# The opening of an encoder layer: first projections in halves of 256 tokens, V's first unit and its fill ahead of the first scores

## The reference, cut to what matters

```python
hn = rmsnorm(x, ln_mix_pre[i])
q, k, v = jnp.split(hn @ w_qkv, 3, axis=-1)          # 16 heads of 64
for blk in range(seq // Q_BLOCK):
    z = jnp.einsum('bhqd,bhkd->bhqk', q[:, :, t0:t1], k[:, :, :t1]) * scale
    log_stay = jnp.where(before, jax.nn.log_sigmoid(-z), 0.0)
    log_pass = lax.cumsum(log_stay, axis=3, reverse=True) - log_stay
    a = jnp.where(before, jnp.exp(jax.nn.log_sigmoid(z) + log_pass), 0.0)
    outs.append(jnp.einsum('bhqk,bhkd->bhqd', a, v[:, :, :t1]))
x = x + rmsnorm(concat(outs) @ w_o, ln_mix_post[i])
x = x + rmsnorm(swiglu_ffn(rmsnorm(x, ln_ffn_pre[i]), w_gu, w_down), ln_ffn_post[i])
```

## Time and profile before

| what | us |
|---|---|
| median of three runs (1438.04 to 1438.3) | 1438.04 |
| the profiled execution's own time | 1431.42 |
| its span | 1429.6 |
| TensorE busy | 1353.5 (95%) |
| VectorE busy | 720.0 (50%) |
| ScalarE busy | 544.1 (38%) |
| GpSimd busy | 377.8 (26%) |

### The profile page before, as it was taken

One profiled execution on the slowest core, in us unless ns is written; L12 is line 12 of the kernel. 1 busy time (PEld: TensorE's weight loads), 2 busy tenths in 40 slices (PEclk: granted clock), 3 DMA queues, 4 the chain that ended last, 5 costly groups with the idle time before them and its releaser, 6 DMA issues.

```text
span 1429.6 us, 17837 instructions
## 1 busy us (share of the span) xinstructions
PE 1353.5 (95%) x6528; PEld 1121.9 (78%) x6528; DVE 720.0 (50%) x881; ACT 544.1 (38%) x964; POOL 377.8 (26%) x244
## 2 busy tenths in 40 slices
PE   5999999999999967996999999999999999999995
PEld 4788888888888856785788888888888888888884
DVE  6489989899898994323212130313132222313148
ACT  5577767677776762332221112021212111111213
POOL 5111011101111051551252323142323232232326
PEclk9999999999999978997999999999999999999998
DMA  5000000000000032120011101020211111110102
GB/s 191 31 30 16 31 30 30 29 15 30 30 30 15 16 103 74 63 70 0 30 59 44 60 30 59 29 73 15 73 44 53 50 44 44 44 59 29 59 15 118
DMA packets 18335, 66.64 MB, mean 47 GB/s; under 512 B 2032, under 2 KB 2032, under 8 KB 18288
## 3 DMA queue, kind: packets, MB, share of 16 engines
q1 hardware_dynamic: 16560, 59.78, 12.1%
q10 hardware_dynamic: 1728, 6.29, 1.3%
HBM read 61.87 MB, written 4.19 MB: 46 GB/s over the span
## 4 chain that ended last, share of the span: by engine, by line
PE 91%; DVE 6%; ACT 1%; DMA 1%; POOL 0%; issue 0%; POOLq 0%; ACTq 0%; DVEq 0%
PE bank L1152 11%; PE bank L1151 11%; PE bank L1153 11%; PE bank L1001 6%; PE bank L1003 6%; PE bank L1002 6%; PE bank L1199 5%; PE bank L1198 5%; PE bank L1200 5%; PE bank L1102 4%; PE bank L1076 2%; PE bank L1078 2%; PE bank L1122 2%; PE bank L1121 2%; PE bank L1050 2%; PE bank L1052 2%
## 5 line engine op out<-in xcount | busy, mean ns | idle before, releaser
L693 POOL TENSOR_TENSOR w_lo<-raw,w_hi 128x1024 fp32r<-128x1024 f32 x89 | 216.1, 2432 | 746.1 <-ACT w_hi L438 745.9
L1151 PE MATMUL bank<-hnT_hi,w_hi 128*128 128x512 f32 x704 | 277.4, 394 | 2.9 <-DVE hnT_lo L794 2.9
L1152 PE MATMUL bank<-hnT_lo,w_hi 128*128 128x512 f32 x704 | 278.8, 396 | 0.0
L1153 PE MATMUL bank<-hnT_hi,w_lo 128*128 128x512 f32 x704 | 276.4, 393 | 0.0
L934 DVE TENSOR_TENSOR sg<-bank,sg 128x512 f32<-128x512 f32 x44 | 30.4, 692 | 439.3 <-ACT sg L626 439.3
L438 ACT ACTIVATE w_hi<-raw 128x1024 fp32r<-128x1024 f32 x89 | 93.3, 1059 | 404.2 <-PE bank L1153 353.5
L874 DVE TENSOR_TENSOR_SCAN stay<-stay,diag_one 128x256 f32<-128x256 f32 (+7 forms) x128 | 189.8, 1483 | 5.8 <-ACT stay L554 5.8
L948 DVE TENSOR_TENSOR y<-bank,y 128x512 f32<-128x512 f32 x176 | 119.3, 690 | 94.4 <-PE bank L1200 93.1
L1151 PEld LDWEIGHTS bank<-hnT_hi,w_hi 128*128 128x128 f32 x704 | 133.1, 189 | 34.7 <-DVE hnT_lo L794 3.5
L1153 PEld LDWEIGHTS bank<-hnT_hi,w_lo 128*128 128x128 f32 x704 | 133.0, 189 | 29.9
L1152 PEld LDWEIGHTS bank<-hnT_lo,w_hi 128*128 128x128 f32 x704 | 132.9, 189 | 29.2
(11 more groups left out here) (97 smaller groups left out, 2018.5 us busy)
## 6 DMA issues: line engine op xcount, KB each, us to landing
raw<-in_units SPq DMA_DIRECT2D x98, 512.0 KB, 3.2
acc<-in_x SPq DMA_DIRECT2D x8, 512.0 KB, 8.6
x_in<-in_x ACTq DMA_DIRECT2D x8, 512.0 KB, 3.4
out<-y SPq DMA_DIRECT2D x7, 512.0 KB, 2.6
g_pre_s<-in_mix_pre ACTq DMA_DIRECT2D x1, 512.0 KB, 5.5
g_post_t<-in_mix_post ACTq DMA_DIRECT2D x1, 512.0 KB, 4.2
g_ffn_t<-in_ffn_pre ACTq DMA_DIRECT2D x1, 512.0 KB, 3.7
g_out<-in_ffn_post ACTq DMA_DIRECT2D x1, 512.0 KB, 3.8
```

Source lines behind the costliest of these rows:

```text
L693: nc.gpsimd.tensor_tensor(w_lo[slot], raw[:, raw_slot, :], w_hi[slot].bitcast(F32), ALU.subtract).then_inc(w_ready, 1)
L1151: nc.tensor.matmul(bank_ap, wh, hnT_hi[:, kt, cols], start=(kt == 0), stop=False)
L1152: nc.tensor.matmul(bank_ap, wh, hnT_lo[:, kt, cols], start=False, stop=False)
L1153: mm = nc.tensor.matmul(bank_ap, wl, hnT_hi[:, kt, cols], start=False, stop=(kt == KT - 1))
```

## The change

1. SyncE issues `g_pre_s` behind the first tile (it was ScalarE's first instruction), k's unit behind it and q's behind the second tile; the other six tiles follow.
2. ScalarE splits k's unit after the first tile's squares (was the fourth's), q's after the third's (was the seventh's) and V's after the sixth's (was after the third projection).
3. The low parts of these three units are made by VectorE, after it has scaled tiles 0, 2 and 6, and no longer by GpSimd.
4. Each of the four first projections is done in two halves of 256 tokens (`project_first`), 24 matmuls of 256 columns each; `FIRST_PARTS` and `FIRST_TILES` are rewritten for pairs (projection, half), so that a half follows the transposes of tiles 2 to 7 and two follow the last.
5. V's first unit lies in a slot of its own, the chunk buffers `AT_hi` and `AT_lo`, unused until slot 7.
6. In the first step the seven parts of slots 0 to 2 all stand ahead of slot 0's scores.

```diff
--- before.py
+++ after.py
@@ -182,10 +182,16 @@
     return UNIT_OFF[kind] % 2 if first else (UNIT_OFF[kind] + par) % 2
 
 
-def fill_parts(s):
-
-    parts = [("vkq"[n // 16], n % 16 // 8, n % 8) for n in range(PARTS_UPTO[s], PARTS_UPTO[s + 1])]
-    return parts[:1], parts[1:]
+def fill_parts(s, first):
+
+
+
+    upto = PARTS_UPTO[s + 1]
+    if first and s < 3:
+        upto = PARTS_UPTO[3]
+    parts = [("vkq"[n // 16], n % 16 // 8, n % 8)
+             for n in range(PARTS_UPTO[3] if first and s in (1, 2) else PARTS_UPTO[s], upto)]
+    return (parts, []) if first and s == 0 else (parts[:1], parts[1:])
 
 
 ACC_END = acc_base(PAIRS - 1) + 2
@@ -207,11 +213,9 @@
 
 FIRST_ACC = [("k", 0), ("q", 1), ("k", 1), ("q", 0)]
 
-FIRST_PARTS = {3: [(0, range(0, 2))], 4: [(0, range(2, KT))], 6: [(1, range(0, 5))],
-               7: [(1, range(5, KT))],
-               NT: [(2, range(KT)), (3, range(KT))]}
-
-FIRST_TILES = [4, 6, 8, 8]
+
+FIRST_PARTS = {2: [(0, 0)], 3: [(3, 0)], 4: [(0, 1)], 5: [(1, 0)], 6: [(2, 0)], 7: [(1, 1)], NT: [(2, 1), (3, 1)]}
+FIRST_TILES = [(2, 4), (4, 6), (6, 8), (2, 8)]
 
 
 
@@ -345,9 +349,11 @@
 
             return k_b[:, par, :] if h else k_a[:, par, :]
 
-        w_hi = [w_hi01[:, 0, :], w_hi01[:, 1, :], w_hi2[:, :], hnT_hi[:, 0, :]]
-        w_lo = [w_lo01[:, 0, :], w_lo01[:, 1, :], w_lo2[:, :], hnT_lo[:, 0, :]]
-        LAST_SLOT = 3
+
+
+        w_hi = [w_hi01[:, 0, :], w_hi01[:, 1, :], w_hi2[:, :], hnT_hi[:, 0, :], AT_hi.rearrange("p a n -> p (a n)")]
+        w_lo = [w_lo01[:, 0, :], w_lo01[:, 1, :], w_lo2[:, :], hnT_lo[:, 0, :], AT_lo.rearrange("p a n -> p (a n)")]
+        LAST_SLOT, FIRST_V_SLOT = 3, 4
 
         x_tile = [sem(f"x_tile{t}") for t in range(NT)]
         raw_in = [sem("raw_in0"), sem("raw_in1")]
@@ -406,12 +412,12 @@
 
         @block.sync
         def _(sp):
-            for t in range(4):
+            for t in range(NT):
                 sp.dma_start(acc[:, t, :], x_tiles[:, t, :]).then_inc(x_tile[t], 16)
-            sp.dma_start(raw[:, 0, :], units[0]).then_inc(raw_in[0], 16)
-            for t in range(4, NT):
-                sp.dma_start(acc[:, t, :], x_tiles[:, t, :]).then_inc(x_tile[t], 16)
-            sp.dma_start(raw[:, 1, :], units[1]).then_inc(raw_in[1], 16)
+                if t == 0:
+                    sp.dma_start(g_pre_s[:, :], g_mix_pre.partition_broadcast(P)).then_inc(gain_in, 16)
+                if t < 2:
+                    sp.dma_start(raw[:, t, :], units[t]).then_inc(raw_in[t], 16)
             for n in range(2, UNITS1):
                 sp.wait_ge(w_ready, n - 1)
                 sp.dma_start(raw[:, n % 2, :], units[unit_row(n)]).then_inc(raw_in[n % 2], 16)
@@ -445,7 +451,6 @@
                 act.wait_ge(t_full, index + 1)
                 nc.scalar.activation(out_ap, in_ap, ACT.Copy).then_inc(t_hi, 1)
 
-            act.dma_start(g_pre_s[:, :], g_mix_pre.partition_broadcast(P)).then_inc(gain_in, 16)
 
 
             def start_hi(t):
@@ -460,10 +465,12 @@
                     act.wait_ge(sq_done, t)
                 nc.scalar.activation(junk_s[:, :], acc[:, t, :], ACT.Square,
                                      accum_out=ss[:, t:t + 1]).then_inc(sq_done, 1)
-                if t == 3:
+                if t == 0:
                     split_hi(0, 0, 0, 16)
-                if t == 6:
+                if t == 2:
                     split_hi(1, 1, 1, 16)
+                if t == 5:
+                    split_hi(2, FIRST_V_SLOT, 0, 32)
                 if t >= 2:
                     start_hi(t - 2)
             start_hi(NT - 2)
...
@@ -704,10 +709,6 @@
             for t in range(NT):
                 pool.wait_ge(sq_done, t + 1)
                 inverse_rms(t, t)
-                if t == 3:
-                    split_lo(0, 0, 0)
-            split_lo(1, 1, 1)
-            split_lo(2, 0, 0)
 
             def step(p, par, first=False, proj=True):
                 for s in range(SLOTS):
@@ -804,6 +805,8 @@
                 nc.vector.memset(q_lo2[OTHER[h], h, :].bitcast(F32), 0.0).then_inc(zeros, 1)
             dve.wait_ge(consts, 5)
             dve.wait_ge(gain_in, 16)
+
+            FIRST_SPLIT = {0: (0, 0), 2: (1, 1), 6: (2, FIRST_V_SLOT)}
             for t in range(NT + 1):
                 if t < NT:
                     dve.wait_ge(rstd_done, t + 1)
@@ -812,6 +815,11 @@
                     nc.vector.scalar_tensor_tensor(out=hn_s[:, t % 2, :], in0=acc[:, t, :],
                                                    scalar=rstd[:, t:t + 1], in1=g_pre_s[:, :],
                                                    op0=ALU.mult, op1=ALU.mult).then_inc(hn_ready, 1)
+                if t in FIRST_SPLIT:
+                    n, slot = FIRST_SPLIT[t]
+                    dve.wait_ge(w_hi_ready, n + 1)
+                    nc.vector.tensor_tensor(w_lo[slot], raw[:, n % 2, :], w_hi[slot].bitcast(F32),
+                                            ALU.subtract).then_inc(w_ready, 1)
                 if t:
                     norm_lo(2 * t - 2, t - 1, 0)
                     norm_lo(2 * t - 1, t - 1, 1)
@@ -991,6 +999,26 @@
 
         @block.tensor
         def _(pe):
+            def project_first(n, b):
+
+                kind, c = FIRST_ACC[n]
+                slot = "kq".index(kind)
+                first_col = (0, 6 * P)[b] if (kind, c) == ("q", 0) else 2 * P * ((1 if kind == "q" else 2 * c) + b)
+                cols = slice(first_col, first_col + 2 * P)
+                dst = FIRST_ACC_B[n][:, 2 * P * b:2 * P * (b + 1)]
+                pe.wait_ge(w_ready, slot + 1)
+                pe.wait_ge(t_lo, 2 * FIRST_TILES[n][b])
+                for kt in range(KT):
+                    wh = w_hi[slot][:, kt * P:(kt + 1) * P]
+                    wl = w_lo[slot][:, kt * P:(kt + 1) * P]
+                    nc.tensor.matmul(dst, wh, hnT_hi[:, kt, cols], start=(kt == 0 and b == 0), stop=False,
+                                     skip_group_check=True)
+                    nc.tensor.matmul(dst, wh, hnT_lo[:, kt, cols], start=False, stop=False, skip_group_check=True)
+                    mm = nc.tensor.matmul(dst, wl, hnT_hi[:, kt, cols], start=False,
+                                          stop=(kt == KT - 1 and b == 1), skip_group_check=True)
+                if b:
+                    mm.then_inc(acc_full, 1)
+
             def project_tiles(kind, c, slot, kts, dst):
 
                 out_ap = dst[:, :].rearrange("p (g n) -> p g n", n=2 * P) if kind == "q" and c == 0 else dst[:, :]
@@ -1020,12 +1048,8 @@
                     pe.wait_ge(hn_ready, t + 1)
                     for half in range(2):
                         transpose_norm(2 * t + half, hn_s[:, t % 2, :], half)
-                for n, kts in FIRST_PARTS.get(t, []):
-                    kind, c = FIRST_ACC[n]
-                    unit = "kq".index(kind)
-                    pe.wait_ge(w_ready, unit + 1)
-                    pe.wait_ge(t_lo, 2 * FIRST_TILES[n])
-                    project_tiles(kind, c, unit, kts, FIRST_ACC_B[n])
+                for n, b in FIRST_PARTS.get(t, []):
+                    project_first(n, b)
 
             def fill(p, par, first, parts, proj):
 
@@ -1036,7 +1060,8 @@
                             pe.wait_ge(w_ready, n + 1)
                         if kt == 0:
                             pe.wait_ge(acc_free, index + c - 1)
-                        project_tiles(kind, c, unit_parity(par, first, kind), range(kt, kt + 1), ACCB[c])
+                        slot = FIRST_V_SLOT if first and kind == "v" else unit_parity(par, first, kind)
+                        project_tiles(kind, c, slot, range(kt, kt + 1), ACCB[c])
 
             def wo_part(t, c, j):
 
@@ -1079,7 +1104,7 @@
                                                   skip_group_check=True)
                         mm.then_inc(av_done, 1)
                     if not tail:
-                        fill(p, par, first, fill_parts(s)[0], proj)
+                        fill(p, par, first, fill_parts(s, first)[0], proj)
                     for n, kind, at in t_slot(s):
                         g = t_index(p, n)
                         if kind == "v" and not tail:
@@ -1121,7 +1146,7 @@
                             nc.tensor.matmul(dst, q_hi2[:, h, qs], kk[:, a:e], start=True, stop=False)
                             mm = nc.tensor.matmul(dst, q_lo2[:, h, qs], kk[:, a:e], start=False, stop=True)
                         mm.then_inc(z_full, 1)
-                        fill(p, par, first, fill_parts(s)[1], proj)
+                        fill(p, par, first, fill_parts(s, first)[1], proj)
                     elif s in WO_TAIL:
                         if s == 1:
                             pe.wait_ge(w_ready, UNITS1)
```

2 lines of the change are left out of this document (removed).

## The result

The changed kernel takes 1422.37 us (median of 4, 1418.91 to 1423.21), the kernel before beside it 1438.12 (median of 4, 1438.04 to 1438.3): ratio 0.9886, 95% interval 0.9869 to 0.9903, 15.7 us less. I had forecast faster, but 1432.1, and the time lies under my range. The profiled execution of after is 1421.83 (span 1419.9), 0.5 under its median, where that of before was 6.6 under its own. So the spans differ by 9.7 and the medians by 15.7, and the difference between these two is the heart of this case.

The account below looks back on a forecast made before the run. The opening was taken to be bound by TensorE waiting for VectorE, then a lowered clock. Slot 7 moves from 73.56 to 67.7, 5.9 us earlier, so 1438.04 becomes 1432.1; range 1430 to 1435, with rivals 1429.3 to 1436.8.

Parts of the forecast that it names:

- I carry the difference over: Whole kernel: the median's 6.6 us above the profiled time was kept, giving 1438.04 - 5.9 = 1432.1.
- I let everything shift: Behind slot 7: everything ends earlier by the opening's 5.9 us, with nothing taking it back.
- less the slow clock: -3.0: First scores to slot 7: 15 matmuls that lasted 6.4 us take 3.4 with the clock up.
- Tile 2's transposes: Opening, TensorE: they start at 19.2 us, where tile 3's had started at 19.06.
- The six tiles and eight halves: Opening, TensorE: transposes 1.94 + 5.2, half projections 22.5, and 2.1 us lost to the slow clock.
- the length of the slow stretch: Opening, from 19.2 on: low clock as long as after 55.98, 6.2 to 6.4 us, costing 2.1.
- from the first scores to slot 7: TensorE: 17.6 us before becomes 11.8, with holes bounded by 0 and 3, so slot 7 at 67.7.
- sum for the row work: VectorE, from the first scores to slot 7: 11.6 us against TensorE's 11.8, level, no wait, no margin.
- The late clock: Opening rival: one more cold half with its transposes costs 3.2 us; gain 2.7, time 1435.3; chance 13%.
- The late row work: Rival at slot 7: it waits 2 to 3 us for VectorE; gain 3.4, time 1434.6; chance 10%.
- Half-wide matmuls paced by the weight load: First projections rival: 0.19 us a matmul costs 14.0 more; kernel slower by 8, 1446; chance 5%.
- The change not doing what it says: Rival: V parts wait, idle time moves ahead of them, clock falls; 0.5 to 1 us gained, 1437.3; 4%.

Follow-up runs that it names:

- b0_again: The kernel before, unchanged, timed against itself with a profile of its own: 1435.99 us, ratio 0.9994, profiled 1436.02.
- e7: The changed kernel with first projections whole again in the old places, plus 14 unused 16-column matmuls ahead of the first transposes: 1425.4 us, ratio 0.9939.
- e3: The changed kernel with V's fill in the old places, one part ahead of the first scores and two behind: 1424.4 us, ratio 0.9928.
- e11: The changed kernel with the three first low parts back on GpSimd: 1422.26 us, ratio 0.9919.
- e8: The kernel before with 14 unused bf16 matmuls of 16 columns at the head of TensorE's program: 1428.62 us, ratio 0.9948.
- e6: The changed kernel with the first projections whole again and in the old places: 1434.97 us, ratio 1.0.
- e9: The changed kernel with 32 unused bf16 matmuls of 16 columns at the head of TensorE's program: 1430.92 us, ratio 0.9964.
- e2: The kernel before with only the seven V parts put ahead of the first scores: 1432.15 us, ratio 0.9971.

## Why the prediction was wrong

**The step that failed** first is the last one of the sum: "The median is 6.6 above the profiled time for reasons the profile doesn't show; I carry the difference over." The difference belongs to the kernel before and not to the chip. By their times, before's executions mostly fetch the program of the attention loop again; the one shown did not. (Only profiled executions show it directly; for the others it is inferred.) b0_again, an execution with the refetch, stands 4.6 in span above the shown one: -3.8 opening, +8.0 between slot 7 and w_o, +0.4 behind. The change adds 96 matmuls with 96 weight loads ahead of the loop, and where the loop then lies it is fetched once. After's median stands 0.5 above its profiled time. Carrying 6.6 over was wrong by 6.1 of the 9.7 us by which I missed. The other 3.7 are, within 0.1, 2.8 in the opening, 1.6 between slot 7 and w_o, and -0.6 behind it. They matter too: with 6.1 off, my range would have been 1423.2 to 1430.7, and 1422.37 still lies under it.

**"I let everything shift" behind slot 7.** For the two executions I compared this was nearly right: slot 7 came 8.7 earlier, the end 9.7. For the medians it was wrong. Between b0_again and after the spans differ by 14.3: 4.9 in the opening, 9.6 from slot 7 to w_o, -0.2 behind it. The 1.4 left to the medians' 15.7 are within what executions of one kernel differ by.

**The opening.** Its mechanism was right and its size too small: 8.7 against 5.9. Tile 2's transposes came 0.6 early. The six tiles and eight halves took 1.9 less. Nearly all of that is the clock, which was up from 21.9 on, not from 25.4, because I took the length of the slow stretch from another place of the trace, where TensorE had a different past: (25.4 - 21.9) / 2 = 1.8 us. The wait of 0.2 ahead of V's parts did not come, and from the first scores to slot 7 it took 11.54 instead of 11.8. V's parts took 0.1 more. Before rounding that is 2.8. (The recorded sum for the row work, 0.46 + 0.2 + 2.2 + 8.6, is 11.5 and not 11.6; it changes nothing.) Against an execution of before whose clock did not fall, 3.0 of this gain aren't there: the term "less the slow clock: -3.0" exists only where the wait ahead of the first scores brings the clock down, in some executions. That the profile shown to me was one of them was luck; against b0_again the opening gained 4.9.

**By part of the change.** Halves 3.0 by the medians, 4.9 at slot 7 (e7 against after). The fill of three slots 2.0 by the medians, 3.5 at slot 7 (e3 against after). The low parts on VectorE nothing that shows (e11). The layout 8.7 to 9.6 by the medians (e8 against before, e6 against e7, and 8.5 the other way in e9), 7.7 to 9.5 from slot 7 to w_o. Of the 15.7, taking 8.5 to 9.6 off for the layout leaves an estimate of 6.1 to 7.2 for the opening; halves and fill alone sum to 5.0 by the medians and 8.4 at slot 7. Before's own median differs by up to 1.9 from round to round, so these shares are rough. Slot 7 shows one thing more. From b0_again (69.7) the fill alone leads to 67.6 (e2). With the new order of transfers and splits on top, but whole projections, it is 71.0 (e6): without the halves that order costs 3.4. The halves then lead to 64.9, 6.1 earlier. So the early weights are worth having only because the halves use them.

**The rivals.** The late clock: it came early. The late row work: level, as forecast, no wait. Half-wide matmuls paced by the weight load: no, 0.12 apart while their loads take 0.19, which overlap. The change not doing what it says: it did. None of the four looked past the opening. One on the other side of the range, that the 6.6 us are something the change can remove, was missing.

**What stays open.** The rule by which the layout acts is known only as far as a period goes. Shift 0 has the holes in three of four traces (the shown execution of before is the exception), 256 has them in its one, and 28, 56, 192 and 320 don't have them in their nine. A period of 256 or 128 fits, but no run with 128 tells these two apart, and which places within it are good is not known. (After also has two semaphore instructions more ahead of the loop, which my count of shifts leaves out.) Nor do I know why one kernel has them in some executions only: before's own times run from 1425.51 to 1439.12 over all runs, e8's from 1423.27 to 1431.31, e9's from 1421.95 to 1434.19. A layout seems to make the refetch likely or unlikely, no more.

## What to carry to other kernels

When a kernel's profiled execution is faster than its median by more than its executions differ, don't carry the difference over: take a second profile and subtract the two, stage by stage. In a long kernel with a loop, look for idle time "<-issue" at the loop's back edge (where it jumps to its start), read how long the branch takes, and count the instruction transfers. If they go on in later iterations, a few cheap instructions ahead of the loop are an edit to try by itself (0.5 us bought 8.7 here). And an edit that changes the number of instructions ahead of a loop is to be compared with one that adds as many dummies, before its gain is put down to its idea.
